# A 31-tap depthwise convolution on TensorE: four-tap stacks on column strips in place of 64x64 quadrants and VectorE taps

## The reference, cut to what matters

```python
def conformer_conv(h, w_pw1, b_pw1, w_dw, b_dw, ln_g, ln_b, w_pw2, b_pw2):
    u = h @ w_pw1 + b_pw1
    a, gate = jnp.split(u, 2, axis=-1)
    u = a * jax.nn.sigmoid(gate)
    u = causal_dwconv_2(u, w_dw, b_dw)      # 31 taps, each of 1024 channels by itself
    u = jax.nn.silu(layernorm(u, ln_g, ln_b))
    return u @ w_pw2 + b_pw2
```

## Time and profile before

| | |
|---|---|
| median of three runs | 1113.43 us (1112.86 to 1113.97) |
| the profiled execution | 1115.66 us |
| its span | 1113.5 us |
| mean granted clock of TensorE | 0.986 |
| PE busy | 1069.3 us (96%) |
| DVE busy | 774.6 us (70%) |
| ACT busy | 527.9 us (47%) |
| POOL busy | 155.6 us (14%) |

### The profile page before, as it was taken

The page is one execution under the profiler, slowest core; times in us unless marked ns, Lnnn a source line. Parts: engine busy times, 40 slices in busy tenths (PEclk is TensorE's granted clock), DMA queues, the critical chain, the costliest instruction groups (busy, mean ns, idle before and its releaser), DMA issues. The chain is left out here.

```text
span 1113.5 us, 22850 instructions
## 1 busy us (share of the span) xinstructions
PE 1069.3 (96%) x8733; PEld 1010.6 (91%) x8733; DVE 774.6 (70%) x1249; ACT 527.9 (47%) x908; POOL 155.6 (14%) x192
## 2 busy tenths in 40 slices
PE   8999889799999999998999999998997999999998
PEld 7999669699999999876999999998995799999998
DVE  5876657565557767885777767777876666776775
ACT  6443455544443446225644444454645555444442
POOL 0060020011114310002010010032013600001000
PEclk9999899899999999999999999999999999999999
DMA  8563206255564563420556555555631035555551
GB/s 329 164 189 98 86 11 190 76 160 185 185 189 151 184 195 114 115 77 1 171 171 197 180 188 172 188 154 152 228 115 52 1 109 175 181 198 176 182 190 56
DMA packets 46436, 165.24 MB, mean 148 GB/s; under 512 B 5152, under 2 KB 6176, under 8 KB 46240
## 3 DMA queue, kind: packets, MB, share of 16 engines
q1 hardware_dynamic: 45216, 163.24, 46.1%
q10 hardware_dynamic: 1152, 1.05, 0.4%
HBM read 162.17 MB, written 1.05 MB: 147 GB/s over the span
## 5 line engine op out<-in xcount | busy, mean ns | idle before, releaser
L1485 DVE TENSOR_TENSOR WL<-WR,WH 128x1024 fp32r<-128x1024 f32 x302 | 380.2, 1274 | 147.0 <-ACT WH L1235 140.6
L846 PE MATMUL acc<-XH,WH 128*128 128x256 f32 x1392 | 403.6, 290 | 7.7 <-DVE VA L1502 2.8
L848 PE MATMUL acc<-XH,WL 128*128 128x256 f32 x1392 | 394.8, 284 | 0.0
L847 PE MATMUL acc<-XL,WH 128*128 128x256 f32 x1392 | 394.5, 283 | 0.0
L1235 ACT ACTIVATE WH<-WR 128x1024 fp32r<-128x1024 f32 x302 | 312.0, 1050 | 119.6 <-PE acc L848 85.8
L846 PEld LDWEIGHTS acc<-XH,WH 128*128 128x128 f32 x1392 | 267.4, 192 | 12.5 <-DVE WL L1485 8.3
L847 PEld LDWEIGHTS acc<-XL,WH 128*128 128x128 f32 x1392 | 267.2, 192 | 1.0
L848 PEld LDWEIGHTS acc<-XH,WL 128*128 128x128 f32 x1392 | 267.1, 192 | 0.0
L846 PE MATMUL big<-UH,WH 128*128 128x256 f32 x608 | 170.9, 281 | 0.9 <-POOL UL L1970 0.6
L847 PE MATMUL big<-UL,WH 128*128 128x256 f32 x608 | 169.6, 279 | 0.0
L848 PE MATMUL big<-UH,WL 128*128 128x256 f32 x608 | 169.6, 279 | 0.0
(11 more groups left out here) (293 smaller groups left out, 1295.2 us busy)
## 6 DMA issues: line engine op xcount, KB each, us to landing
WR<-weights SPq DMA_DIRECT2D x302, 512.0 KB, 3.6
X<-x_t SPq DMA_DIRECT2D x4, 256.0 KB, 6.5
MEM<-mem_t SPq DMA_DIRECT2D x1, 1024.0 KB, 10.1
result_t<-X SPq DMA_DIRECT2D x4, 256.0 KB, 2.2
CON<-constants SPq DMA_DIRECT2D x1, 896.0 KB, 12.3
CBUF<-KCV ACTq DMA_DIRECT2D x4, 128.0 KB, 5.5
CBUF<-KCV ACTq DMA_DIRECT2D x4, 127.5 KB, 7.1
SML<-small_weights SPq DMA_DIRECT2D x1, 480.0 KB, 14.8
```

The costliest lines, as they stand in the source:

```text
L846: pe.matmul(out, wh, hi, start=start, stop=False, skip_group_check=True)
L847: pe.matmul(out, wh, lo, start=False, stop=False, skip_group_check=True)
L848: return pe.matmul(out, wl, hi, start=False, stop=stop, skip_group_check=True)
L1485: dve.tensor_tensor(WL[:, cs % SPL], WR[:, cs % RAW], WH[:, cs % SPL].bitcast(F32), ALU.subtract).then_inc(w_low, 1)
```

## The change

PE takes all 31 taps, DVE none. A feature tile of 128 channels is taken as four groups g of 32. For each group, ACT issues a transfer that reads the group's 32 rows of UPAD four times, shifted by 0, 1, 2 and 3 tokens, and lays them on the 128 partitions of STK[j % 4, g] (channel times four plus shift), 284 columns each. A matmul with 128 rows and 32 columns then does four taps of 32 channels: its weights are a 128 x 32 matrix with four stacked entries to a column. Eight such passes (`QUADS`) at offsets 0, 4, ..., 28 of STK make 32 taps, of which the last has weight zero. The four groups go to four column strips of 32 of the array, and write partitions 32g to 32g + 31 of one bank. So a feature tile takes 8 x 4 = 32 f32 matmuls, and all eight tiles 256, where there were 288 and 32 with the identity.

The loop runs over single feature tiles: PE does gated(j + 2), taps(j) and, from j = 2, sum_features(j - 2). ACT issues the four transfers of tile j (`stack_shifts`) behind the split of chunk 2j + 4, once up_ready shows tile j, and copies out tile j - 3 behind them, now with the convolution's bias. UPAD has four slots; DVE waits before it writes a slot again until the transfers out of it have landed. POOL's matrices have 1024 columns to a tile where they had 1152. The order of the channels after the convolution, which the host had permuted for the quadrants, is now the plain one.

```diff
-PE_TAPS = 18
+QUADS = (CONV_W + 3) // 4
+STACKED = T + 4 * (QUADS - 1)
+UPS = 4
...
-            def taps(p):
-                pe.wait_ge(sem("up_ready"), 2 * p + 2)
-                pe.wait_ge(sem("diagonals"), 2 * p + 2)
-                if p >= 2:
-                    pe.wait_ge(sem("cx_whole"), 2 * p - 2)
-                halves = [(r, c, slice(64 * r, 64 * r + 64), slice(64 * c, 64 * c + 64)) for r in range(2) for c in range(2)]
-                for i in range(PE_TAPS):
-                    for r, c, rs, cs in halves:
-                        pe.matmul(big[cs, 2 * (p % 2) + r, 0:T], DG[rs, p, i, c, :], UPAD[rs, 2 * p + c, i:i + T],
-                                  start=i == 0, stop=False, skip_group_check=True)
-                pe.wait_ge(sem("part_done"), 4 * p + 4)
-                for a in range(2):
-                    for r, c, rs, cs in halves:
-                        ins = pe.matmul(big[cs, 2 * (p % 2) + r, 0:T], con("ident2")[rs], CD[rs, p % 2, c, a],
-                                        start=False, stop=a == 1, skip_group_check=True)
+            def taps(j):
+                pe.wait_ge(sem(f"stacked{j % UPS}"), 64 * (j // UPS + 1))
+                pe.wait_ge(sem("diagonals"), j + 1)
+                if j >= 4:
+                    pe.wait_ge(sem("cx_whole"), j - 3)
+                for m in range(QUADS):
+                    for g in range(4):
+                        ins = pe.matmul(big[32 * g:32 * g + 32, j % 4, 0:T], DG[:, j, g * QUADS + m, :],
+                                        STK[:, j % UPS, g, 4 * m:4 * m + T], start=m == 0, stop=m == QUADS - 1,
+                                        skip_group_check=True)
                 ins.then_inc(sem("taps_ps"), 1)
...
-            for p in range(4):
-                if p < 3:
-                    gated(2 * p + 2)
-                    gated(2 * p + 3)
-                taps(p)
-                if p >= 1:
-                    sum_features(2 * p - 2)
-                    sum_features(2 * p - 1)
+            for j in range(KD):
+                if j + 2 < KD:
+                    gated(j + 2)
+                taps(j)
+                if j >= 2:
+                    sum_features(j - 2)
...
+            def conv_out(j):
+                act.wait_ge(sem("taps_ps"), j + 1)
+                act.activation(CX[:, j], big[:, j % 4, 0:T], ACT.Identity, bias=vec("b_dw", j)).then_inc(sem("cx_whole"), 1)
+
+            def stack_shifts(j):
+                act.wait_ge(sem("up_ready"), j + 1)
+                if j >= UPS:
+                    act.wait_ge(sem("taps_ps"), j - UPS + 1)
+                for g in range(4):
+                    x = UPAD[32 * g:32 * g + 32, j % UPS, 0:STACKED]
+                    shifts = bass.AP(x.tensor, x.offset, [list(x.ap[0]), [1, 4], [1, STACKED]])
+                    act.dma_start(STK[:, j % UPS, g, :], shifts).then_inc(sem(f"stacked{j % UPS}"), 16)
...
                 sp.to(C0 + 2 * j + 2 + AHEAD)
-                if j % 2 == 1 and j >= 3:
-                    conv_out((j - 3) // 2)
-            conv_out(3)
+                stack_shifts(j)
+                if j >= 3:
+                    conv_out(j - 3)
+            for j in range(KD - 3, KD):
+                conv_out(j)
...
             dve.memset(UPAD[:, :, 0:CONV_W - 1], 0.0)
+            dve.memset(UPAD[:, :, CONV_W - 1 + T:], 0.0)
...
+                if j >= UPS:
+                    dve.wait_ge(sem(f"stacked{j % UPS}"), 64 * (j // UPS))
...
-            for p in range(5):
-                if p < 4:
-                    gate_half(2 * p)
-                if p >= 1:
-                    taps(p - 1, 0, 3)
...
+            for j in range(8):
+                gate_half(j)
+                value_half(j)
+                gated(j)
...
             def diagonals(j):
-                w = VEC[:, VCOL["w_dw"] + CONV_W * j:VCOL["w_dw"] + CONV_W * j + PE_TAPS]
-                pool.tensor_tensor(DG[:, j // 2, :, j % 2, :], con("ident2").unsqueeze(1).broadcast_to([P, PE_TAPS, 64]),
-                                   w.unsqueeze(2).broadcast_to([P, PE_TAPS, 64]), ALU.mult).then_inc(sem("diagonals"), 1)
+                w = VEC[:, VCOL["w_dw"] + 4 * QUADS * j:VCOL["w_dw"] + 4 * QUADS * (j + 1)]
+                pool.tensor_tensor(DG[:, j], con("ident4").unsqueeze(1).broadcast_to([P, 4 * QUADS, 32]),
+                                   w.unsqueeze(2).broadcast_to([P, 4 * QUADS, 32]), ALU.mult).then_inc(sem("diagonals"), 1)
```

More of the change, by code:

```diff
@@ L48 @@
            ("mem_g", 8), ("ff_g", 8), ("final_g", 8), ("mix2_g", 16), ("ffn2_g", 16), ("b_pw1", 16),
-           ("w_dw", 8 * CONV_W), ("b_dw", 8), ("ln_g", 8), ("ln_b", 8), ("b_pw2", 8),
+           ("w_dw", 8 * 4 * QUADS), ("b_dw", 8), ("ln_g", 8), ("ln_b", 8), ("b_pw2", 8),
            ("q_g", 1), ("kc_g", 1), ("ks_g", 1), ("kw_g", 1), ("fconv", 2 * UP_TILES * 4),
@@ L60 @@
           ("block_ones", 128), ("rope", 128), ("neg_causal", 128), ("cmp_neg", 32), ("cmp_01", 32),
-          ("v_mask", 128), ("ident2", 64), ("cos", T), ("sin", T)]
+          ("v_mask", 128), ("ident4", 32), ("cos", T), ("sin", T)]
 CCOL = {}
@@ L163, in program @@
         OS = QT
[L165 to L168, removed]
+        B = group([("SG", [P, 2, T], F32), ("AT", [P, 2, T], F32), ("UP", [P, UPS, STACKED + 4], F32),
+                   ("CX", [P, KD, T], F32), ("MU", [P, T], F32), ("STK", [P, UPS, 4, STACKED], F32),
+                   ("DG", [P, KD, 4 * QUADS, 32], F32)])
+        SG, AT, UPAD, CX, MU, STK, DG = (B[n] for n in ("SG", "AT", "UP", "CX", "MU", "STK", "DG"))
         C = group([("GU", [P, 2, T], F32), ("UH", [P, 2, T], F32R), ("UL", [P, 2, T], F32R),
@@ L1829, in gated @@
                 dve.wait_ge(sem("gate_done"), j + 1)
-                dve.scalar_tensor_tensor(UPAD[:, j, CONV_W - 1:], AT[:, j % 2], vec("b_pw1", 2 * j + 1), SG[:, j % 2],
+                if j >= UPS:
+                    dve.wait_ge(sem(f"stacked{j % UPS}"), 64 * (j // UPS))
+                dve.scalar_tensor_tensor(UPAD[:, j % UPS, CONV_W - 1:CONV_W - 1 + T], AT[:, j % 2], vec("b_pw1", 2 * j + 1), SG[:, j % 2],
                                          ALU.add, ALU.mult).then_inc(sem("up_ready"), 1)
-            own = CONV_W - PE_TAPS
@@ L1834, in _ @@
[L1834 to L1855, removed]
@@ L2046, in _constants @@
         "v_mask": ((i[:, None] % 32) // 16 == i[None, :] // 64) & (i[:, None] % 16 < N_CMP),
-        "ident2": np.concatenate([np.eye(64), np.eye(64)]), "cos": cos, "sin": sin,
+        "ident4": np.repeat(np.eye(32), 4, axis=0), "cos": cos, "sin": sin,
     }
@@ L2062 @@
     heads = np.concatenate([np.arange(64 * h, 64 * h + 64) for h in order])
-    conv_out = np.array([P * (2 * p + c) + 64 * r + i for p in range(4) for r in range(2) for c in range(2) for i in range(64)])
     pw1 = a["conv_w_pw1_2"][0]
@@ L2090 @@
               _outer(a["w_xo"][0], 8).reshape(4, 2, P, 512).transpose(0, 2, 1, 3).reshape(4, P, CH),
-              ff(a["w_ff1"][0], a["w_ff2"][0]), _outer(pw1[:, gate_then_a], 16), _outer(a["conv_w_pw2_2"][0][conv_out], 8),
+              ff(a["w_ff1"][0], a["w_ff2"][0]), _outer(pw1[:, gate_then_a], 16), _outer(a["conv_w_pw2_2"][0], 8),
               ffn(a["ffn_w_up_2"][0], a["ffn_w_down_2"][0]),
@@ L2100, in taps, with stacked @@
         return w.reshape(w.shape[0], tiles, P).transpose(2, 1, 0).reshape(P, -1)
+    def stacked(w):
+        w = np.concatenate([w, np.zeros((4 * QUADS - CONV_W, D), w.dtype)]).reshape(QUADS, 4, 8, 4, 32)
+        return w.transpose(4, 1, 2, 3, 0).reshape(P, -1)
     def pairs(pe):
@@ L2115 @@
         "b_pw1": _features(a["conv_b_pw1_2"][0][gate_then_a], 16),
-        "w_dw": taps(a["conv_w_dw_2"][0], 8), "b_dw": _features(a["conv_b_dw_2"][0], 8),
-        "ln_g": _features(a["conv_ln_g_2"][0][conv_out], 8), "ln_b": _features(a["conv_ln_b_2"][0][conv_out], 8),
+        "w_dw": stacked(a["conv_w_dw_2"][0]), "b_dw": _features(a["conv_b_dw_2"][0], 8),
+        "ln_g": _features(a["conv_ln_g_2"][0], 8), "ln_b": _features(a["conv_ln_b_2"][0], 8),
         "b_pw2": _features(a["conv_b_pw2_2"][0], 8), "q_g": twice(a["nsa_q_norm_2"][0]), "kc_g": twice(a["nsa_kc_norm_2"][0]),
```

## The result

The changed kernel takes 1103.29 us (median of four runs, 1101.43 to 1104.0), beside 1113.14 us for the kernel before on the same chip: a ratio of 0.9921 [0.9904, 0.9939]. The forecast was 1109.5 with a range from 1106.0, so the sign was right and the size was not. Two repetitions gave 0.9939 [0.9923, 0.9954] and 0.9922 [0.9903, 0.9942], gains of 6.8 and 8.7 us. The mean of the three ratios is 0.9927, some 8.1 us of 1113, where 3.9 us were forecast.

The account below looks back on a forecast made before the run. PE, busy 96% of the span, was taken as the bound. Taps, tiles, sums, hand-overs, ACT's hold and stack waits sum to 66.8 us against 70.6, 3.9 less: 1113.43 - 3.9 = 1109.5 us, range 1106.0 to 1115.5.

Parts of the forecast that it names:

- Taps: PE's convolution matmuls: 512 records at 54.3 ns, four strips abreast, 27.8 us after, the main term at -7.0 us.
- rival (b): PE's taps: strips do not run four abreast; the gain is gone from 61.9 ns a record, two abreast 1137.3 us; chance 0.13.
- The rule of the Trainium skill: PE's weight loads: overlap a running matmul only if row groups differ; would put taps 98 us above the forecast; chance 0.01.
- the estimate worked out from that page's speedup of three column tiles: PE's taps: three column tiles at 2.38 times one, an estimate of 79% of full rate and 1116.8 us; beside rival (b).
- Hand-overs: PE's changes between tiles, taps and sums: 0.5 us a round, eight rounds for four, 4.0 us for 2.0, +2.0 us.
- DVE's sums: PE's waits for DVE's sums (CD), 0.54 us in each of three rounds; their removal was worth 1.6 us.
- rival (d): DVE was what mattered, so freeing it brings back far more than 1.6 us; given no chance of its own.
- Landing: Transfers into STK land 6.4 to 9.9 us after the first issue; PE waits 0.2 us before taps(0), 1.2 before taps(7).
- rival (c): Stacks land late, so taps(0) and taps(7) wait; gain gone at 11.1 us, 1119.3 us at 14; chance 0.15.
- ACT's hold: ACT's four transfer issues, 2.7 us, delay its later work, so PE waits 1.3 us (0 to 2.6) before weight tile 5.
- Rival (a): Convolution's stage gains more: hand-overs cost 0.38 us each (-1.0), both stacks land in time (-1.4), 1107.1 us; chance 0.10.
- Edits at nothing: POOL's smaller matrices, bias in ACT's copy, second memset, eight more vector columns: covered, under 0.1 us if any cover failed.

Follow-up runs that it names:

- the experiment with the order: The changed kernel with a tile's 32 matmuls reordered, all eight passes of one strip before the next strip's; one run of 1164.09 us.
- the experiment with shorter sums: The kernel before with four of DVE's 13 taps left out in each tile, PE's work the same; one run of 1108.2 us.

## Why the prediction was wrong

**Taps: right.** The forecast was 54.3 ns a record with the strips four abreast. They run at 54 ns a record, 56.1 with both ends of a group of 64, which is 28.7 us for eight tiles against 27.8 (+0.9 us). Of rival (b) nothing is left: its 61.9 ns are far off, and the experiment with the order shows the overlap itself as worth 60 us. The rule of the Trainium skill that I weighed against the change ("TensorE: Matmul & The Clock Gate", Part 3, what overlaps and what doesn't) is not borne out: with loads of 110 ns into shared rows the records keep the quadrants' pace. Nor is the estimate worked out from that page's speedup of three column tiles (with 512 columns of data, where there are 256 here).

**Hand-overs: the step that failed most inside the stage, a term too large.** I took 0.5 us for each round and eight rounds for four, +2.0 us. A round of two tiles and taps now takes 9.54 us (437.43 to the next taps at 446.97); without 2 x 2.88 and 3.59 there are 0.19 left, 0.26 in the last one, 1.6 us in all instead of 4.0. The 0.5 was a mixture: 0.23 us was the tail of the wait for DVE, which the change removes. I subtracted the 0.54 that the profile prints from the round, and called the remainder a price of the switch. The last round, which has no wait, showed 0.38 and should have been the measure for all; I used it as an end only. Where taps end and a hand-over begins is a matter of counting: 3.59 us are 0.11 more than 64 x 54.3 ns, and 0.11 and 0.19 make the same 0.30 us a round that the quadrants show without the wait. So the price of the switch is 0.3 us, not 0.5; the forecast had 31.8 us for taps and hand-overs together, and they took 30.3.

**DVE's sums: right in kind, a third too small.** 2.3 us, not 1.6, by the experiment with shorter sums. So rival (d) had a little of the truth, and far less than DVE's 41 us.

**Landing: too late by half.** I took 0.2 and 1.2 us of wait, from 9.9 us between an issue and a use. The interval held nothing but the issues and the transfers: by the trace of the kernel before, the fourth landed 7.87 us after its own issue, at 758.58, and DVE started at 758.61. The line of the slower half of those transfers, beside the earlier trace rows:

```profile
DMA to landing us min/median/max: 6.0/7.1/7.9
```

The new ones land 3.2 to 4.5 us after their own issue, where the quickest old one took 4.4. So they are really quicker, from half the partitions; which of the differences between the two does it was not tested. With landings 5.4 to 6.4 us after the first issue no taps wait, and rival (c) is gone.

**ACT's hold: right in place and cause, a little small.** 1.3 us forecast; 1.86, 1.33 and 2.08 printed, 1.6 to 2.3 by the starts. The first four issues take 3.24 us, for one took 1.24. In the other two executions they take 2.71 and 3.45, and the hold by the starts follows: 1.6, 2.1 and 2.3 us for issues of 2.7, 3.2 and 3.5. So at the 2.7 us forecast the hold is 1.6, and what lies over that is the length of the last issue.

The stage by these terms: taps 28.7, tiles 28.8, sums 3.5, hand-overs 1.6, hold 2.1, together 64.7 us from the point that was 440.83, where the forecast had 66.8 (and 65 to 69 as the sign of being right) and the trace has 64.65 (step 31 at 403.21, plus 32.14, to 500.00). That is 5.9 us less than before for 3.9 forecast. Rival (a), which lowered just these terms, was the better forecast of the stage.

**POOL's matrices: the step that failed outside it.** "Edits at nothing", "less than 0.1 us". They gave 1.7 us. POOL is idle 86% of the time, and I read that as cover. But what an instruction of POOL costs is not POOL's time: it held DVE's split, and the trace of the kernel before had it to see, a split of 3.0 us against a median of 1.22. The smaller build of the change shortens each hold by 0.2 us. Since the first 3.2 us of delay cost PE nothing in either kernel, a tenth less POOL work took away 60% of PE's loss. The change was not made for this, and the gain from it is luck as far as the forecast goes.

The 3.9 us forecast, 2.1 more in the stage and these 1.7 make 7.7; the two feed-forwards add 0.1 us each, for which I have no cause. The rest of the first comparison, 9.9 us against the pooled 8.1, is within the spread between runs of one kernel.

## What to carry to other kernels

Before an instruction of an idle engine is costed at nothing, look in the trace at what the other engines' instructions last while it runs; a maximum of 3.0 us over a median of 1.2 in one line is a price. A wait that the profile prints can be less than what it costs (0.54 us for 0.77 here), so compare whole rounds with and without it, and don't book the remainder on something else. Where column strips share their rows, issue one pass on every strip before the next pass.

## What the runs showed of the hardware that I had not expected

- A f32 matmul of 128 rows and 32 columns over 256 columns of data: 216 ns a record alone, 54 ns with four strips in turn; at a change of strip four records start within 30 ns of the one before.
- A DVE subtraction with two inputs in SBUF all but stands still while POOL multiplies out of SBUF: 3.00 us for 1.22, started 0.2 us behind a build of 2.12 us.
- Transfers from 32 partitions of SBUF to 128, 142 KB each, landed in 3.2 to 4.5 us (median 3.9) in stretches in which all transfers together moved 125 to 208 GB/s, and cost ACT's queue 0.63 us each (median; one 1.24). Those of much the same size from 64 partitions (L544, L545) took 4.4 to 7.9 us.
- Two executions of one program lay 5.0 us apart at step 17, with a granted clock of 0.79 against 1.00 between 8 and 16 us. Eight more columns in one table made the kernel 0.37% slower, with PE's matmuls further apart at a granted clock of 1.00, which stays unexplained.
